# Three norms and the ends of the products in front of them, reordered bank by bank, by tile and by feature; a bias summed by GpSimd

## The reference

```
h = rms_norm(x, g)                         # x / sqrt(mean(x*x) + 1e-6) * g, over the 1024 features
x = x + square(relu(h @ w1)) @ w2          # the end of each layer of block 1
h = rms_norm(x, norm1_g) * (1 + sc1) + sh1 # in front of w_in_2 (norm 4) and, with sc2, sh2, of PEER (norm 5)
scores = q @ k / 8 + bias                  # local attention; -inf where the mask forbids
x = x + g1 * (mixed @ w_out)               # the end of the mixer of block 2
```

## Time and profile before

| what | value |
|---|---|
| timed runs | median 1564.53 us of 3, 1562.4 to 1565.94 |
| profiled execution, its own time | 1564.93 us |
| its span | 1563.1 us |
| mean granted TensorE clock | 0.976 of full |
| TensorE busy | 1470.7 us (94%) |
| VectorE busy | 1143.2 us (73%) |
| ScalarE busy | 781.3 us (50%) |
| GpSimd busy | 320.4 us (20%) |
| HBM read | 344.22 MB, 221 GB/s over the span |

### The profile page before, as it was taken

The page is one execution under the profiler, slowest core; times in us unless marked ns, Lnnn a source line. Parts: engine busy times, 40 slices in busy tenths (PEclk is TensorE's granted clock), DMA queues, the critical chain, the costliest instruction groups (busy, mean ns, idle before and its releaser), DMA issues.

```text
span 1563.1 us, 28782 instructions
## 1 busy us (share of the span) xinstructions
PE 1470.7 (94%) x11224; PEld 1359.6 (87%) x11224; DVE 1143.2 (73%) x2258; ACT 781.3 (50%) x1574; POOL 320.4 (20%) x381
## 2 busy tenths in 40 slices
PE   7788999997899999979889999999999999999998
PEld 6566998676879988869779999999998999999997
DVE  4585995585857889857664799377777768888887
ACT  5685885554255545546444211344333256666664
POOL 6510001000000000001000000378888711111110
PEclk9999999999999999989799999999999999999999
DMA  6204554443158989835135466799999988898884
GB/s 235 84 28 143 162 166 137 127 153 123 45 175 264 320 295 344 304 104 163 54 112 173 162 202 202 244 347 362 359 354 327 338 299 304 301 309 303 302 308 145
DMA packets 95429, 347.14 MB, mean 222 GB/s; under 512 B 10608, under 2 KB 10736, under 8 KB 95040
## 3 DMA queue, kind: packets, MB, share of 16 engines
q1 hardware_dynamic: 67824, 245.50, 46.7%
q0 software_dynamic: 19408, 71.36, 12.8%
q10 hardware_dynamic: 8064, 28.45, 5.2%
HBM read 344.22 MB, written 1.05 MB: 221 GB/s over the span
## 4 chain that ended last, share of the span: by engine, by line
PE 73%; DVE 12%; DMA 5%; ACT 4%; issue 3%; POOL 3%; ACTq 0%; DVEq 0%
PE ps L560 72%; DVE arena L1175 5%; DMA arena<-in_u_rows,arena 2%; DVE w_lo L1175 2%; ACT arena L1970 2%; DMA arena<-in_v_rows,arena 1%; POOL arena L2795 1%; POOL arena L2806 1%; DVE arena L1181 1%; DVE arena L1178 1%; ACT w_hi L1973 1%; ACT arena L1973 1%; DVE act_hi_lo L1175 0%; PE ps L831 0%; DVE arena L1307 0%
## 5 line engine op out<-in xcount | busy, mean ns | idle before, releaser
L1175 DVE TENSOR_TENSOR w_lo<-arena,w_hi 128x512 fp32r<-128x512 f32 x680 | 458.0, 687 | 240.1 <-ACT w_hi L1973 236.4
L1973 ACT ACTIVATE w_hi<-arena 128x512 fp32r<-128x512 f32 x680 | 421.8, 627 | 326.4 <-PE ps L560 287.6
L560 PE MATMUL ps<-act_hi_lo,w_hi 128*128 128x256 f32 (+1 forms) x2496 | 565.0, 317 | 3.8 <-ACT w_hi L1973 2.6
L560 PE MATMUL ps<-arena 128*128 128x192 f32 (+10 forms) x5232 | 530.2, 284 | 37.5 <-DVE arena L1178 15.8
L560 PEld LDWEIGHTS ps<-arena 128*128 128x128 f32 (+2 forms) x5232 | 494.9, 165 | 69.0 <-issue 30.1
L560 PE MATMUL ps<-act_hi_lo,w_lo 128*128 128x192 f32 (+1 forms) x1760 | 465.6, 265 | 0.0
L560 PEld LDWEIGHTS ps<-act_hi_lo,w_hi 128*128 128x128 f32 x2496 | 422.7, 191 | 7.6 <-ACT w_hi L1973 4.7
L560 PE MATMUL ps<-w_hi,act_hi_lo 128*128 128x512 f32 (+2 forms) x960 | 314.8, 400 | 29.3 <-DVE w_lo L1175 10.2
L560 PEld LDWEIGHTS ps<-act_hi_lo,w_lo 128*128 128x128 f32 x1760 | 338.0, 192 | 0.0
L560 PEld LDWEIGHTS ps<-w_hi,act_hi_lo 128*128 128x128 f32 x960 | 184.8, 194 | 78.0 <-issue 27.2
L1175 DVE TENSOR_TENSOR arena<-arena 128x512 f32<-128x512 f32 (+16 forms) x308 | 193.0, 634 | 50.6 <-ACT arena L1970 36.0
(11 more groups left out here) (91 smaller groups left out, 658.5 us busy)
## 6 DMA issues: line engine op xcount, KB each, us to landing
arena<-in_w_ff SPq DMA_DIRECT2D x128, 512.0 KB, 4.1
arena<-in_peer_u SPq DMA_DIRECT2D x128, 512.0 KB, 5.3
arena<-in_peer_v SPq DMA_DIRECT2D x128, 512.0 KB, 5.5
arena<-in_w_ada ACTq DMA_DIRECT2D x48, 512.0 KB, 5.1
arena<-in_w_glu SPq DMA_DIRECT2D x16, 512.0 KB, 4.2
arena<-in_peer_wq SPq DMA_DIRECT2D x16, 512.0 KB, 3.9
arena<-in_w_in SPq DMA_DIRECT2D x12, 512.0 KB, 4.5
arena<-in_w_conv SPq DMA_DIRECT2D x12, 512.0 KB, 3.6
```

The lines of the kernel that those rows point to most:

```text
L560: return e.matmul(o, l, r, start=start, stop=stop)
L1175: return e.tensor_tensor(o, a, b, op)
L1973: return e.activation(o, a, ACT.Copy)
```

## The change

The end of both feed-forwards. `down_last` (new, TensorE) takes the last two units, which are four pieces, by bank: for each tile and each half first m = 0, then m = 1. It holds all four pieces until the second tile, and signals each bank.

```diff
+        def down_last(name, j, side):
+
+            hi, lo = HQ[j % 4]
+            e.wait_ge(*alo_cut[name, j])
+            pieces = []
+
+            def piece(i):
+                while len(pieces) <= i:
+                    pieces.append(chunk(name))
+                return pieces[i]
+            for t in range(2):
+                at_t = slice(t * 128, (t + 1) * 128)
+                for hf in range(2):
+                    for m in range(2):
+                        ins = three(pb(2 + 2 * t + hf, 512), (hi[:, m, at_t], lo[:, m, at_t]), piece(2 * m + hf),
+                                    False, m == 1)
+                        if t == 1 and (hf, m) == (0, 0):
+                            ins.then_inc(*w_used())
+                        elif t == 1 and (hf, m) == (1, 0):
+                            w_used()
+                            ins.then_inc(w_used()[0], 2)
+                        elif t == 1 and (hf, m) == (1, 1):
+                            ins.then_inc(*w_used())
+                        elif m == 1:
+                            ins.then_inc(*mm_done(name, t, hf))
+                    next(side, None)
 
         def down(name, units, layer, ada=None, side=iter(())):
             for j in range(units // 2):
+                if j == units // 2 - 1:
+                    down_last(name, j, side)
+                    continue
```

```diff
                 for hf in range(2):
                     bk, xs = 2 + 2 * t + hf, xr[:, t, 512 * hf:512 * hf + 512]
                     if t == 0 and hf == 0:
                         e.wait_ge(*stats["norm_rs", s])
+                    if (t, hf) == (1, 1):
+                        e.wait_ge(w_used.sem, end[name])
+                    else:
+                        e.wait_ge(*mm_done[name, t, hf])
                     stt(xs, pb(bk, 512), stat(f"norm{s}", 3)[:, t:t + 1], xs, ALU.mult,
                         ALU.add).then_inc(bank[bk].sem, 1)
+                    if (t, hf) == (1, 0):
+                        norm_scale(after, 0)
+            half_mean(after, slice(1, 2))
+            norm_scale(after, 1)
 
 ...
+        def norm_scale(s, t):
+            ss = stat(f"norm{s}", 5)[:, t:t + 1]
+            e.wait_ge(*rooted["norm", s, t])
+            e.reciprocal(ss, ss).then_inc(*stats("norm_rs", s, t))
+            e.wait_ge(*stats["norm_rs", s, t])
+            ts(scale_at(s)[:, t, :], ident, ss, None, ALU.mult).then_inc(*diagonal("norm", s, t))
+
+        def half_mean(s, tiles):
+
+            ss = stat(f"norm{s}", 5)[:, 2 + tiles.start:2 + tiles.stop]
+            e.wait_ge(*squared["norm", s, "half"])
+            ts(ss, ss, 1.0 / 1024, EPS, ALU.mult, ALU.add).then_inc(*stats("norm half", s))
 ...
+        def rows_roots(s, scratch, name):
+
+            st = stat(f"norm{s}", 5)
+            act(st[:, 4:5], sm("ones")[:, 0:1], ACT.Sqrt)
+            e.wait_ge(*bank[2][name])
+            e.wait_ge(*bank[3][name])
+            act(V(scratch, 1024), xr[:, 0, :], ACT.Square, accum_out=st[:, 0:1]).then_inc(*squared("norm", s, 0))
+            root(s, 0)
+            e.wait_ge(*bank[4][name])
+            act(V(scratch + 1024, 512), xr[:, 1, 0:512], ACT.Square,
+                accum_out=st[:, 3:4]).then_inc(*squared("norm", s, "half"))
+            e.wait_ge(*bank[5][name])
+            act(V(scratch, 512), xr[:, 1, 512:1024], ACT.Square, accum_out=st[:, 1:2]).then_inc(*squared("norm", s, 1))
+            root(s, 1)
```

`norm_scale` waits for `root`, which takes the mean and the root of one tile (ScalarE). TensorE's `norm` turns all blocks of tile 0, then those of tile 1. VectorE and ScalarE go feature block by feature block, and the three cuts that `down` leaves out now stand here (in front of S5, three `chunk()` calls stand ahead of `s5()` on both engines):

```diff
-                bank[4 + n].take(e, "norm", s)
-                for t in range(2):
+            for t in range(2):
+                e.wait_ge(*diagonal["norm", s, t])
+                for n in range(4):
+                    if t == 0:
+                        bank[4 + n].take(e, "norm", s)
                     for k in range(2):
                         o = (2 * n + k) * 128
-                        ins = mm(pb(4 + n, 2, 2, 128)[:, k, t, :], xr[:, t, o:o + 128], scale_at[:, t, :], True, True)
-                ins.then_inc(*turned("norm", s, n))
+                        ins = mm(pb(4 + n, 2, 2, 128)[:, k, t, :], xr[:, t, o:o + 128], scale_at(s)[:, t, :], True, True)
+                    if t == 1:
+                        ins.then_inc(*turned("norm", s, n))
 ...
+
+            hT = V(20480, 8, 256)
+            chunk()
+            for k in range(8):
+                if k % 2 == 0:
+                    e.wait_ge(*turned["norm", s, k // 2])
+                ins = ts(hT[:, k, :].rearrange("p (t n) -> p t n", t=2), pb(4 + k // 2, 2, 2, 128)[:, k % 2],
+                         gain[:, k:k + 1], shift[:, k:k + 1], ALU.mult, ALU.add)
+                if k % 2 == 0:
+                    ins.then_inc(*shifted("norm", s, k))
+                else:
+                    ins.then_inc(bank[4 + k // 2].sem, 1)
+                if k > 0:
+                    low(HL[:, k - 1, :], hT[:, k - 1, :], HH[:, k - 1, :], "norm", s, k - 1)
+                if k == 2 or k == 4:
+                    chunk()
+            low(HL[:, 7, :], hT[:, 7, :], HH[:, 7, :], "norm", s, 7)
 ...
+            hT = V(20480, 8, 256)
+            chunk()
+            for k in range(8):
+                e.wait_ge(*(shifted["norm", s, k] if k % 2 == 0 else bank[4 + k // 2]["norm", s]))
+                copy(HH[:, k, :], hT[:, k, :]).then_inc(*ahi_cut("norm", s, k))
+                if k == 1 or k == 3:
+                    chunk()
```

```diff
+                if b == 0:
+                    e.wait_ge(*diagonal["norm", 2, 0])
+                    e.wait_ge(*diagonal["norm", 2, 1])
                 bank[bk].take(e, "s5_u", b)
                 for p in range(8):
                     f = 256 * b + 32 * p
                     for t in range(2):
                         for jj in range(4):
-                            ins = mm(pb(bk, 8, 64)[32 * jj:32 * jj + 32, p, 32 * t:32 * t + 32], hn[:, t, f:f + 32],
-                                     ident4[:, jj, :], True, True)
+                            ins = mm(pb(bk, 8, 64)[32 * jj:32 * jj + 32, p, 32 * t:32 * t + 32], xr[:, t, f:f + 32],
+                                     select[:, t, :, jj], True, True)
```

```diff
+        def lin_tok_by_tiles(name, n, banks, ready, *use):
+
+            yield from lin_tok(name, n, banks, ready, *use, ks=range(4))
+            pieces = []
+            for t in range(2):
+                at_t = slice(t * 128, (t + 1) * 128)
+                for k in range(4, 8):
+                    if t == 0:
+                        pieces.append(chunk(name))
+                        ready(k)
+                    ins = three(pb(banks[t], n), (HH[:, k, at_t], HL[:, k, at_t]), pieces[k - 4], False, k == 7)
+                    if t == 1:
+                        ins.then_inc(*w_used())
+                    elif k == 7:
+                        ins.then_inc(*mm_done(name, "first tile"))
+                    if k % 2 == 1:
+                        yield
 
 ...
+        mix_out("w_out", ((6, 7), (2, 3)), gb[:, 0, :], both(gens + [first_half()], 16))
+        for t in range(2):
+            if t == 0:
+                e.wait_ge(*mm_done["w_out", "first tile"])
+            else:
+                e.wait_ge(w_used.sem, end["w_out"])
+            add_to_x(2 + t, t, 1, ("w_out", 1), gb[:, 0, :])
+            norm_scale(5, t)
         gsc = stat("gain2", 8)
```

Bias and mask: VectorE's add and ScalarE's two DMA issues behind norm 4 are gone. GpSimd does both early, behind the S5 outputs, and local attention waits for it:

```diff
+        e.wait_ge(*mm_done["s5_y", 3])
+        e.dma_start(V(WB, 2048), T["wbias"]).then_inc(win_in, 16)
+        e.dma_start(V(WB + 2048, 256), T["wmask"]).then_inc(win_in, 16)
+        e.wait_ge(*got_win)
+        for h in range(8):
+            ins = tt(wb[:, h, :], wb[:, h, :], V(WB + 2048, 256), ALU.add)
+        ins.then_inc(*win_p("bias"))
 
```

More of the change, by code:

```diff
@@ L590, in wait @@
             def wait(k):
-                if k // 2 not in waited:
-                    waited.add(k // 2)
-                    e.wait_ge(*alo_cut["norm", s, k // 2])
+                if k not in waited:
+                    waited.add(k)
+                    e.wait_ge(*alo_cut["norm", s, k])
             return wait
@@ L1395, in done @@
                         add_to_x(banks[j][t], t, j, (name, j), gate)
-                weave(lin_tok(done), side)
+                if (name, j) == ("w_out", 1):
+                    for _ in range(5):
+                        chunk()
+                        next(side, None)
+                else:
+                    weave(lin_tok(done), side)
         ada_at = dict(n=0)
@@ L1469, in ffn @@
                 ada_end()
-            e.wait_ge(w_used.sem, end[f"ff2_{layer}"])
+            run(side)
+            name, after = f"ff2_{layer}", s + 1
             for t in range(2):
@@ L2180, in mixer0, with mix_out @@
             run(steps)
-        def mix_out(side=iter(())):
-            for j in range(2):
-                weave(lin_tok(), side)
+        def mix_out(side=iter(()), left=0):
+            for n in range(16 - left):
+                chunk()
+                next(side, None)
         ada_at = dict(n=0)
@@ L2534, in scalar_program @@
         ffn(0, x_ready, s5_tables())
-        def x_ready(t):
```

(8 more changed lines are left out.)

128 lines of the change are left out of this document (39 added, 89 removed).

## The result

| | before | after |
|---|---|---|
| median of all timed runs | 1568.13 us of 10 | 1547.74 us of 10 |
| ratio after to before | | 0.9873, 95% interval 0.9846 to 0.9900 |
| profiled execution, its own time | 1564.93 us | 1547.22 us |
| its span | 1563.1 us | 1545.4 us |
| mean granted clock | 0.976 | 0.987 |

The account below looks back on a forecast made before the run. TensorE, busy 94% of the span, was taken as the bound, so only its idle or low-clock time could fall. 3.1 + 9.6 + 1.1 + 0 = 13.8 us off 1564.53 gave 1550.7 us, own range 1547.5 to 1554.5, 8-in-10 range 1546.5 to 1557.5.

Parts of the forecast that it names:

- Part 1: Norm before S5: TensorE starts at E+2.45, not E+5.6 (E: end of last matmul before a norm); 3.1 us gained.
- Part 2: Norm before the second block (norm 4), with w_qkv and its bias wait: 9.6 us gained, bounds 6.2 to 11.5.
- Part 3: Norm before PEER (norm 5), with peer_wq; S = E+4.35: 1.1 us gained, bounds -2 to +2.5.
- GpSimd's sum: Start of the GLU: eight GpSimd adds for bias and mask cost 0 us, bounds 0 to 1.5.
- Rival A: Four more low clock stretches of 1.5 us around the three norms: 1556.7 us; chance 0.13.
- B: Only the bias wait and its clock count, 8.8 us; cuts eat the earlier diagonals: 1555.7 us; chance 0.11.
- C: TensorE falls to half clock behind the second norm, through w_qkv and convolution; slower, 1570.7 us; chance 0.03.
- D: SyncE requests later w_qkv units late, so the wait returns elsewhere: 3 us, 1553.7; counted within the forecast's 0.70.
- the rest: Row of the stage table for stages outside those listed: 0 us predicted.

Follow-up runs that it names:

- again: The kernel after once more, nothing edited: 1553.59 us against 1568.53 of the kernel before, ratio 0.9898.
- again_2: The kernel after once more, nothing edited, in another group: 1547.23 us, ratio 0.987 to the kernel before.
- norms_only: The kernel after with bias and mask loaded and summed behind norm 4, as in the kernel before: 1557.7 us, ratio 0.9944 to before.
- w_out_whole: The kernel after with the second half of w_out in its old order: 1553.3 us, ratio 0.9911 to the kernel before.
- by_piece: The kernel after with the last four pieces of both feed-forwards in their old order, each piece for both tiles: 1553.6 us, ratio 0.9907 to before.
- fourth_early: The kernel after with the fourth and fifth pieces behind a norm cut one place earlier, among the features: 1546.8 us, ratio 0.9865 to before.
- sum_beside_norm: The kernel after with GpSimd's eight adds waiting for norm 4's second diagonal: 1548.87 us, ratio 0.9883 to the kernel before.
- bias_only: The kernel before with GpSimd's early sum of bias and mask and no norm changes: 1555.77 us against 1566.52, ratio 0.9929.
- before_busy: The kernel before with 24 unused matmuls put in front of the piece that waits for the bias: 1565.44 us, ratio 0.9983 to before.

## Why the prediction was right, and where it was small

**Part 1**, 3.1 us. The first S5 matmul came at E+2.53 instead of E+2.45, and the matched matmuls give 3.0 us at the stage's end. The adds take 0.75 instead of 0.68 each (in before the records of the four overlap); with idle time between them that costs only the last. The three cuts moved behind the norm lay in VectorE's wait, as assumed: the distance is 3.1 at S5's first matmul and 3.0 at its end.

**Part 2**, 9.6 us predicted, 10.6 measured, and 12.3 without the low stretch against 11.1. The start at E+4.9 (4.8) and the clock at 1.66 (1.5) came out. Eight turnings took 2.05 us, 0.26 each where I had taken 0.2, which is hidden behind VectorE's first cut. The term that was off is the time per feature: I took 0.95 us from the pair's durations plus gaps. On the chip one feature takes 0.79, a tensor_scalar of 0.54 and a low part of 0.42 whose records overlap. VectorE's timeline in norm 4, the kernel after, where three features follow each other:

```profile
669.54 0.54 DVE L1234 TENSOR_SCALAR arena<-ps,arena 128x256 f32<-128x256 f32 x1
...
670.33 0.54 DVE L1234 TENSOR_SCALAR arena<-ps,arena 128x256 f32<-128x256 f32 x1
...
671.12 0.54 DVE L1234 TENSOR_SCALAR arena<-ps,arena 128x256 f32<-128x256 f32 x1
...
672.66 1.29 DVE L1231 TENSOR_TENSOR w_lo<-arena,w_hi 128x512 fp32r<-128x512 f32 x2
```

And ScalarE's in the same window:

```profile
672.01 1.66 ACT L2045 ACTIVATE w_hi<-arena 128x512 fp32r<-128x512 f32 x3
```

So the fourth piece came at E+12.1 and not E+13.5, and TensorE waited 2.1 us for it, not 3.0; eight features at 0.16 less are 1.3 of these 1.4. The view names ScalarE's high part as the releaser, but the prediction's w_lo fits: TensorE waits for both parts before the piece's first matmul, the high part that began at 672.01 takes 0.61 us, the low part that followed ran from 672.66 for 0.69, to 673.35, and TensorE started at 673.45. What the view named is the high part of a later piece.

**Part 3**, 1.1 us predicted, 2.55 measured, by the same term. The diagonals came at E+0.4 and E+3.3 (predicted E+0.35 and E+3.4). The fourth piece of `peer_wq` started at E+13.0 instead of S+10.1, which was E+14.45, and the pair of units ended at E+14.35 instead of E+15.9. No low clock stretch fell there in after.

**GpSimd's sum**, 0 us predicted and measured, for the wrong reason. "By the trace the sum stays" rested on one cut of 0.69 us under GpSimd operations. Those were of 128x32; under adds of 128x256 the cut takes up to 1.22. The Trainium skill (GPSIMD Engine Reference, Key points) says that GpSimd shares its SBUF interfaces with VectorE and contends with instructions of two SBUF inputs. The trace agrees: 1.21 and 1.22 us against 0.69, and 0.53 unchanged from PSUM. That VectorE's idle half would hide most of it in the GLU, which the prediction worked out for this case, is what happened. Beside norm 4 it cost 1.5 us.

**Rival A**, the clock, gave one low stretch behind norm 4 in after and again and none in again_2. Behind norm 5 it gave none in after and again and one in again_2, as in the other kernels with the new norm 5; there it cost 0.3 us at the end of the pair of units, since TensorE had been waiting anyway. In front of S5 none of the three had one. The priced four did not come together in any of them. **B** is refuted by the stages of after (3.0 at S5, 2.55 at norm 5) and by norms_only, w_out_whole and by_piece: the diagonals and the order of the ends are worth something by themselves. **C** was seen in none of the profiled executions of the changed form. **D**, late requests by SyncE, did not show: no wait of ScalarE on a `w_qkv` DMA stands between E and the half's end.

**The sum.** The stages that the change touches (the GLU's 0.1 with them) gave 16.3 us in after, where 13.8 were predicted: 2.5 more, of which 1.45 from part 3 and 1.0 from part 2, both by the time per feature. A further 1.6 us of the two profiles' distance is a low clock stretch at 32 us in before that no changed line explains. The median's gain of 19.9 is 3.6 above the stages' 16.3, within its interval (from 15.7 on). Where these 3.6 come from is not shown; the last section has a place where single executions differ by as much.

## What to carry to other kernels

When a wait is priced, add what the clock loses behind it: here 5.8 us of standing still cost 3.0 more, and filling the wait with matmuls that nobody needs gave just these back. Behind the wait of 2.1 us it was 1.66 in two executions and nothing in a third. Making the front of a chain earlier pays only if its slowest member isn't a transfer further on (norms_only: 6.5 us earlier, 3.3 gained). When the claim is that two engines don't disturb each other, look for a row with operands as large as those of the change: the small ones here showed nothing of it.

## What the runs showed that I had not expected

The dense last product of PEER runs at one of two rates, at a granted clock of 1.00 in both, with no wait of TensorE's. The windows of the kernel after, of again, and of again_2 in two places (matmuls in the brackets behind the first busy time):

```profile
1300.00:1340.00 40.00, 40.00 (x283) 40.00 (x283) 33.93 (x51) 25.59 (x44) 6.03 (x6) 1.00 0.89 305
```

```profile
1300.00:1340.00 40.00, 40.00 (x278) 40.00 (x277) 33.18 (x50) 24.61 (x43) 7.09 (x6) 1.00 0.88 296
```

```profile
1300.00:1340.00 40.00, 40.00 (x284) 40.00 (x283) 33.32 (x51) 25.28 (x44) 7.39 (x6) 1.00 0.88 307
1400.00:1440.00 40.00, 40.00 (x278) 40.00 (x277) 33.73 (x50) 25.32 (x44) 6.86 (x6) 1.00 0.88 303
```

It is 283 or 284 matmuls in 40 us, or 278 or 279. Read singly, from 1310 to 1313 us, the distances between starts alternate between a short one, 0.085 to 0.089 us in both executions, and a long one. The long one is 0.196 to 0.199 us in after; in again every second is 0.205. again_2 changes from one rate to the other at about 1380 us, within one execution. Five of 283 are 1.8%, so over the 240 us of the stage the slower rate costs 4.3 us, and over again_2's last 165 us 2.9. Against before, from 1308 to 1545 us, again lost 4.5, fourth_early 4.5 and again_2 3.3; after lost nothing. (again and again_2 lost another 1.7 behind that, with a low clock stretch of 3.4 us there.)

What sets the rate no run here shows. The expectation of again_2 named a rival, that the new order itself brings the wander, and it stays open: the slow rate stands, wholly or in part, in five of the eleven profiled executions with the new norms (again, again_2, fourth_early, sum_beside_norm, by_piece) and in none of the three without them (before, bias_only, before_busy). Three are too few to tell. The times speak against it as the whole wander: 19 executions of before in one group run from 1558.32 to 1574.54, as wide as after's 1541.65 to 1558.28.

A second place lies between 748 and 787 us of before, where no changed line is. The stretch that holds the same 184 matmuls in before, after and again_2:

```profile
748.00:787.00 39.00, 33.53 (x184) 28.17 (x183) 21.95 (x59) 17.36 (x43) 1.49 (x2) 0.78 0.18 56
```

```profile
732.70:771.70 39.00, 33.56 (x184) 28.18 (x182) 21.92 (x59) 17.35 (x43) 1.49 (x2) 0.78 0.19 56
```

```profile
733.70:769.10 35.40, 30.54 (x184) 25.19 (x183) 21.82 (x59) 17.11 (x43) 1.49 (x2) 0.86 0.19 61
```

It takes 3.6 us less in again_2, at a mean granted clock of 0.86 instead of 0.78. Before, after, again and before_busy spend 17 us of it at the low clock; the other ten spend 7 to 14, and are 2.7 to 4.7 us faster there than before. So "the rest" in the table is 0.1 because the two executions happened to be alike here. Such differences, and the two rates, are why kernels that differ by 3 us in their stages can't be told apart by a few timed runs.
